# Dilated attention: queries and keys projected with their columns on partitions, instead of projected with tokens on partitions and transposed

## The reference, cut to what matters

```python
DILATED_GROUPS = ((128, 1), (512, 4), (2048, 16))   # window, dilation; N_GROUPS = 3, H_A = 16, DH_A = 64
proj = (h @ w_in).reshape(B, S, N_GROUPS, 3, H_A, DH_A)      # h: rms-normed x
for g, (window, dilation) in enumerate(DILATED_GROUPS):
    o, lse = dilated_group(proj[:, :, g, 0], proj[:, :, g, 1], proj[:, :, g, 2], bias_g, dilation, radius)
wts = jax.nn.softmax(jnp.stack(lses, axis=0), axis=0)
o = jnp.einsum('gbsh,gbshd->bshd', wts, jnp.stack(outs, axis=0))
return o.reshape(B, S, D_A) @ w_out
```

## Time and profile before

| what | value |
|---|---|
| median of 3 runs | 2387.57 us (2387.22 to 2387.86) |
| span of the profiled execution, first to last instruction | 2387.5 us (its own total time is not given; the median stands 0.1 us above this span) |
| PE busy over the span | 2351.7 us, 98% |
| DVE, ACT, POOL busy | 63%, 50%, 12% |
| granted clock of TensorE | 0.999 of full speed on the mean |
| HBM read | 408.31 MB, 171 GB/s over the span |
| matmuls of transposes for q and k in the stage (L2028) | 96 |

### The profile page before, as it was taken

How to read it: one execution, slowest core, us unless ns; L and a number is a source line. 1 busy time by engine, 2 the same in 40 slices (tenths; PEclk the granted TensorE clock), 3 DMA queues, 4 the chain that set the end, 5 groups by cost and what they waited for, 6 DMA issues and landing times.

```text
span 2387.5 us, 34279 instructions
## 1 busy us (share of the span) xinstructions
PE 2351.7 (98%) x13900; PEld 2020.1 (85%) x13900; DVE 1511.0 (63%) x2307; ACT 1195.5 (50%) x1794; POOL 283.9 (12%) x247
## 2 busy tenths in 40 slices
PE   9999999999999999999999999999999999999999
PEld 8987778779979977777899887788998887888987
DVE  6555567776555658666665677756665687656654
ACT  4444454454444446444544565555554555554543
POOL 1100010000000000000001121434110122333000
PEclk9999999999999999999999999999999999999999
DMA  7755644466566656544666654445666554445554
GB/s 229 209 194 175 172 125 136 148 187 183 186 194 177 186 185 197 173 134 151 184 186 204 203 177 143 124 126 183 186 199 206 181 170 131 121 144 172 183 189 145
DMA packets 263278, 411.66 MB, mean 172 GB/s; under 512 B 13770, under 2 KB 129370, under 8 KB 263120
## 3 DMA queue, kind: packets, MB, share of 16 engines
q1 hardware_dynamic: 256256, 389.59, 53.2%
q0 software_dynamic: 6432, 19.28, 3.1%
q10 hardware_dynamic: 432, 0.59, 0.1%
HBM read 408.31 MB, written 1.10 MB: 171 GB/s over the span
## 4 chain that ended last, share of the span: by engine, by line
PE 85%; DVE 8%; ACT 4%; issue 1%; POOL 1%; DMA 0%; SPq 0%; ACTq 0%; DVEq 0%
PE banks L1926 16%; PE banks L1928 16%; PE banks L1927 16%; PE banks L1952 9%; PE banks L1961 9%; PE banks L1953 9%; DVE w_lo L2517 2%; ACT w_hi L2205 2%; PE banks L2015 1%; PE banks L2075 1%; PE banks L2028 1%; DVE probs L2712 1%; PE banks L1909 1%; PE banks L1910 1%; PE banks L1915 1%
## 5 line engine op out<-in xcount | busy, mean ns | idle before, releaser
L2517 DVE TENSOR_TENSOR w_lo<-w_raw,w_hi 128x1024 fp32r<-128x1024 f32 x688 | 838.9, 1225 | 618.1 <-ACT w_hi L2205 616.9
L2205 ACT ACTIVATE w_hi<-w_raw 128x1024 fp32r<-128x1024 f32 (+2 forms) x744 | 777.8, 1049 | 534.6 <-PE banks L1928 379.5
L1926 PE MATMUL banks<-w_hi,xt_hi 128*128 128x512 f32 (+2 forms) x1056 | 432.3, 409 | 7.0 <-DVE xt_lo L2545 3.6
L1952 PE MATMUL banks<-xt_hi,w_hi 128*128 128x256 f32 x1728 | 426.5, 283 | 4.7 <-DVE w_lo L2517 3.1
L1953 PE MATMUL banks<-xt_hi,w_lo 128*128 128x256 f32 x1728 | 425.2, 283 | 0.0
L1928 PE MATMUL banks<-w_hi,xt_lo 128*128 128x512 f32 (+2 forms) x1056 | 413.3, 391 | 0.0
L1927 PE MATMUL banks<-w_lo,xt_hi 128*128 128x512 f32 (+2 forms) x1056 | 412.4, 391 | 0.0
L1952 PEld LDWEIGHTS banks<-xt_hi,w_hi 128*128 128x128 f32 x1728 | 326.6, 189 | 6.6 <-DVE w_lo L2517 3.4
L1953 PEld LDWEIGHTS banks<-xt_hi,w_lo 128*128 128x128 f32 x1728 | 326.7, 189 | 0.0
L1926 PEld LDWEIGHTS banks<-w_hi,xt_hi 128*128 128x128 f32 x1056 | 198.9, 188 | 52.3 <-DVE w_lo L2517 9.0
L1961 PE MATMUL banks<-xt_lo,w_hi 128*128 128x256 f32 x1728 | 243.0, 282 | 0.0
(11 more groups left out here) (438 smaller groups left out, 3042.4 us busy)
## 6 DMA issues: line engine op xcount, KB each, us to landing
w_raw<-in_w_mlp SPq DMA_DIRECT2D x128, 512.0 KB, 3.7
w_raw<-in_w_in SPq DMA_DIRECT2D x104, 512.0 KB, 3.7
w_raw<-in_ffn_w_gate SPq DMA_DIRECT2D x88, 512.0 KB, 3.9
w_raw<-in_ffn_w_up SPq DMA_DIRECT2D x88, 512.0 KB, 4.2
w_raw<-in_ffn_w_down SPq DMA_DIRECT2D x88, 512.0 KB, 3.6
w_raw<-in_attn_w_in SPq DMA_DIRECT2D x72, 512.0 KB, 3.8
w_raw<-in_ret_w_in SPq DMA_DIRECT2D x64, 512.0 KB, 3.8
w_raw<-in_ret_w_out SPq DMA_DIRECT2D x16, 512.0 KB, 3.8
```

The costliest lines, as they stand in the source:

```text
L1926: pe.matmul(bank, xh, wh, start=(c == 0), stop=False)
L1952: pe.matmul(out[f], hi[:, cols], xh, start=(c == 0), stop=False)
L2205: act.activation(k.w_hi[i % SPLIT][:, 0:m], k.raw[i % RAW][:, 0:m], ACT.Copy).then_inc(*ev.mark(k.w_hi_made, ("w_hi", i)))
L2517: dve.tensor_tensor(lo, raw, hi.bitcast(F32), ALU.subtract).then_inc(*ev.mark(k.w_lo_made, ("w_lo", i)))
```

## The change

Queries and keys of all three groups are projected with `column_pair` (two blocks of 256 columns, four tiles in all): the weights are now the stationary operand, and each tile is 24 matmuls that stream 256 tokens, so the bank holds columns on partitions and tokens along it. One bank holds a block. The row scale is then a value per element along the bank, so a 128x256 tile `row_wide` of it is made once for the stage, by PE and ACT, from the ordered row scales. The new step `evac_columns`, on DVE alone, multiplies bank by `row_wide` and writes `da_qt` (two instructions per block, with the tokens reversed inside the classes) or `da_kt` (one instruction per block). The transposes, their copies and the row buffers are gone, and the freed room holds a third pair of q/k buffers. Values are projected as before. The new evictions stand behind the split of the block's last tile in the plan; `row_order` and `row_wide` stand behind tile 3.

```diff
--- before.py
+++ after.py
@@ -669,6 +669,17 @@
             yield from self.block(xt, w, rows, start + c0, m, first, then=leave)
         return made
 
+    def column_pair(self, w, c0):
+
+        nk = TILE // SEQ
+        bs = [self.new_block(self.xt, 0, DC, SEQ) for _ in range(BLOCK // SEQ)]
+        view = w.rearrange("(k p) n -> p k n", p=P)
+        for k0 in range(0, DC, nk):
+            for n, b in enumerate(bs):
+                at = c0 + n * SEQ
+                yield from self.tile(Tile(view[:, k0:k0 + nk, at:at + SEQ], nk, SEQ, b, k0), "mm_columns")
+        return bs
+
     def pause(self, tiles, polls=16):
         until = len(self.tiles) + tiles
         for _ in range(polls):
@@ -1119,8 +1130,8 @@
         a = self.a
         self.feed(order="classes")
         self.step("masks_seen")
-        q, k = self.put("da_q", 0, [P, HALVES, D]), self.put("da_k", 8, [P, HALVES, D])
-        pairs = [(self.put(f"da_qt{n}", at, [P, DC, SEQ]), self.put(f"da_kt{n}", at + 8, [P, DC, SEQ])) for n, at in enumerate((16, 72))]
+        pairs = [(self.put(f"da_qt{n}", at, [P, DC, SEQ]), self.put(f"da_kt{n}", at + 8, [P, DC, SEQ])) for n, at in enumerate((16, 72, 0))]
+        self.row_wide_of[self.st] = self.tables[0].rearrange("p (o a) h d -> p o (a h d)", o=1)
         vs = [self.put(f"da_v{n}", 32 + 8 * n, [P, HALVES, D]) for n in range(2)]
         outs = self.da_outs = [self.tok, self.put("da_o1", 48, [P, HALVES, D])]
         heads_n = NG * H_A
@@ -1136,13 +1147,31 @@
             while any(name not in got for name in names):
                 yield IDLE
 
-        def columns(g, n, dst, after, c0):
+        def columns(g, n, c0):
+            after = got["dense"] if g == 2 else []
+
             def leave(b):
                 for half in range(HALVES):
-                    self.step("evac", Evac(b, half, self.by_turns(), dst[:, half, c0:c0 + BLOCK], list(after)))
+                    self.step("evac", Evac(b, half, self.by_turns(), vs[g % 2][:, half, c0:c0 + BLOCK], list(after)))
 
             b = yield from self.block(self.xt, w_in, D, (3 * g + n) * D + c0, BLOCK, then=leave)
-            got["qkv"[n], g, c0] = [("evac", b.uid, half) for half in range(HALVES)]
+            got["v", g, c0] = [("evac", b.uid, half) for half in range(HALVES)]
+
+        def turned_columns(g, n, c0):
+            after = [("bias_stored",)] if g == 1 else []
+            bs = yield from self.column_pair(w_in, (3 * g + n) * D + c0)
+            if not ordered:
+                order_rows()
+            for m, b in enumerate(bs):
+                self.step("evac_columns", st, b, pairs[g][n][:, (c0 + m * SEQ) // P:(c0 + (m + 1) * SEQ) // P, :], n == 0, after)
+            got["qk"[n] + "t", g, c0] = [("evac", b.uid) for b in bs]
+
+        ordered = []
+
+        def order_rows():
+            ordered.append(st)
+            self.step("row_order", st, self.new())
+            self.step("row_wide", st, [])
 
         def in_order(g, kinds):
             if g == NG - 1:
@@ -1154,42 +1183,13 @@
                 if g == NG - 1:
                     self.act_share = 3
                 for n, c0 in in_order(g, 3):
-                    after = []
-                    if n < 2 and g:
-                        yield from need(("qk"[n] + "t", g - 1, BLOCK))
-                        after = [got["qk"[n] + " read", g - 1]]
-                    if n == 2 and g == 2:
-                        yield from need("dense")
-                        after = got["dense"]
-                    yield from columns(g, n, (q, k, vs[g % 2])[n], after, c0)
+                    if n < 2:
+                        yield from turned_columns(g, n, c0)
+                    else:
+                        if g == 2:
+                            yield from need("dense")
+                        yield from columns(g, n, c0)
             self.xt_after = [self.last_tile()]
-
-        def turned(g, n, c0):
-            z, zt = (q, k)[n], pairs[g % 2][n]
-            yield from need(("qk"[n], g, c0))
-            last = (g, n, c0) == (NG - 1, 1, BLOCK)
-            if not last:
-                yield from self.pause(1)
-            after = [] if g == 0 else [("bias_stored",)]
-            if g == 2:
-                yield from need("dense")
-                after = got["dense"]
-            made = self.turn_heads(lambda half, c: z[:, half, c * P:(c + 1) * P], zt, DC // 2, got["qk"[n], g, c0], after, n == 0, first=c0 // P)
-            if last:
-                made = drive(made)
-                yield
-            else:
-                made = yield from made
-            got["qk"[n] + "t", g, c0] = made
-            got["qk"[n] + " read", g] = self.heads_read
-
-        def turns():
-            for _ in range(2):
-                yield
-            self.step("row_order", st, self.new())
-            for g in range(NG):
-                for n, c0 in in_order(g, 2):
-                    yield from turned(g, n, c0)
 
         def made(g, c0):
             return got["qt", g, c0] + got["kt", g, c0]
@@ -1220,7 +1220,7 @@
             c0, quick = first * DH_A, (g, first) == (NG - 1, OCT)
             yield from need(("qt", g, c0), ("kt", g, c0))
             at = slice(g * H_A + first, g * H_A + first + OCT)
-            o = Oct(self.new(), g, first, *pairs[g % 2], vs[g % 2], nmax[:, at, :], den[:, at, :], self.stat(2 * OCT), made(g, c0), [])
+            o = Oct(self.new(), g, first, *pairs[g], vs[g % 2], nmax[:, at, :], den[:, at, :], self.stat(2 * OCT), made(g, c0), [])
             got["oct", g, first] = o
             while before() and before().passed < 3:
                 yield IDLE
@@ -1311,7 +1311,7 @@
             yield from dense()
             yield from octs()
 
-        side = self.beside(turns(), attended())
+        side = self.beside(attended())
         drive(projections(), side, finish=False)
         self.x_read = self.xt_after[0]
         drive(self.last_normed(out_t, w_out, D, 1.0, lambda c: c in ready), side)
@@ -1964,6 +1964,34 @@
             if not last:
                 mm.then_inc(*ev.mark(k.pe_done, ("tile", i)))
 
+        if what == "mm_columns":
+            i, = of
+            t = k.tiles[i]
+            b, hi, lo = t.block, k.w_hi[i % SPLIT], k.w_lo[i % SPLIT]
+            if t.k0 == 0:
+                yield from bank_for("blk", b.uid)
+            bank = banks.held["blk", b.uid]
+            out = [bank[:, f * SEQ:(f + 1) * SEQ] for f in range(2)]
+            q.wait_ge(*(yield from ev.of("w_lo", i)))
+            for j in range(t.nk):
+                c = t.k0 + j
+                for half in range(HALVES):
+                    q.wait_ge(*(yield from ev.of(*b.xt.event_hi(half, c))))
+                xh, _ = b.xt.whole(c)
+                for f in range(2):
+                    cols = slice(j * SEQ + f * P, j * SEQ + (f + 1) * P)
+                    pe.matmul(out[f], hi[:, cols], xh, start=(c == 0 and f == 0), stop=False, skip_group_check=True)
+                    pe.matmul(out[f], lo[:, cols], xh, start=False, stop=False, skip_group_check=True)
+            for j in range(t.nk):
+                c = t.k0 + j
+                for half in range(HALVES):
+                    q.wait_ge(*(yield from ev.of(*b.xt.event(half, c))))
+                _, xl = b.xt.whole(c)
+                for f in range(2):
+                    cols = slice(j * SEQ + f * P, j * SEQ + (f + 1) * P)
+                    mm = pe.matmul(out[f], hi[:, cols], xl, start=False, stop=(c == DC - 1 and f == 1), skip_group_check=True)
+            mm.then_inc(*ev.mark(k.pe_done, *([("blk", b.uid)] if t.k0 + t.nk == DC else []), ("tile", i)))
+
         if what == "row_wide":
             st, _ = of
             bank = yield from bank_for("row_wide", st)
@@ -2561,6 +2589,25 @@
                 dve.tensor_copy(e.dst, bank[:, 0:e.block.n]).then_inc(*done)
             give_bank("blk", e.block.uid, e.half)
 
+        if what == "evac_columns":
+            st, b, dst, flip, after = of
+            bank = yield from banks.of("blk", b.uid)
+            q.wait_ge(*(yield from ev.of("blk", b.uid)))
+            q.wait_ge(*(yield from ev.of("row_wide", st)))
+            for e in after:
+                q.wait_ge(*(yield from ev.of(*e)))
+            wide = k.row_wide_of[st]
+            if flip:
+                by_class = lambda z: z.rearrange("p (c s i) -> p c s i", c=2, s=2)
+                for f in range(2):
+                    out = dst[:, f, :].rearrange("p (s c i) -> p c s i", s=2, c=2)[:, :, :, ::-1]
+                    names = [("evac", b.uid), ("bank", "blk", b.uid)] if f else [("evac_part", b.uid)]
+                    dve.tensor_tensor(out, by_class(bank[:, f * SEQ:(f + 1) * SEQ]), by_class(wide[:, 0, :]), ALU.mult).then_inc(*ev.mark(k.dve_done, *names))
+            else:
+                dve.tensor_tensor(dst, bank.rearrange("p (f t) -> p f t", f=2), wide[:, :, :].to_broadcast([P, 2, SEQ]), ALU.mult).then_inc(
```

(5 more changed lines are left out.)

## The result

The changed kernel takes 2391.3 us (median of 20 runs, 2390.8 to 2393.8), the kernel before 2388.6 in the same number of runs (2387.2 to 2389.7). The ratio is 1.0014, interval 1.0009 to 1.0020. So it is 2.7 us slower. That is clear of the noise, but within the 0.2% that I had called the same, and in the range. Its profiled execution took 2393.3 us, with a span of 2391.9, against a span of 2387.5 before.

What follows compares the result with a forecast made beforehand. PE was taken to bound the stage, with DVE's strict queue order setting its waits. 6.8 us of PE work won and given back in waits summed to +1.3 us on 2387.5, so 2388.8 us, range 2381.5 to 2393.5.

Steps and rivals of the forecast that it cites:

- wait for the row scale copy: Behind tile 3, PE waits for DVE's copy of the ordered row scales, queued behind tile 7's split: +2.3 us.
- softmax in the dense heads: Group 1: evictions come when DVE idles, so half of the one 0.9 us softmax wait goes: -0.4 us.
- first oct, scores: Group 2, behind tile 56: PE's scores come three tiles earlier and wait for DVE's k products: +4.2 us.
- first oct, values: Group 2: values wait longer for a copy on ACT, now behind both v evictions: +1.2 us.
- `combine`'s transpose: Group 2's first oct: the q eviction on DVE delaying `combine` goes, and with it the transpose's wait: -0.8 us.
- last oct, scores: Group 2, behind tile 68: k products end 3.9 us after tile 67's slot, tile 68 covers 2.8: +1.1 us.
- its values, v eviction: Last oct: values go behind tile 73, not 72, which covers the wait for the eviction of v: -1.3 us.
- ahead of tile 76: Last transposes now stand directly ahead of tile 76, which needs them; PE waits for the first low part: +2.1 us.
- The new waits: Rival: DVE is not in arrears, so the oct waits and tile 76's don't come; 2380.2 us, chance 0.20.
- The reversed write: Rival: q evictions with reversed tokens cost DVE twice the plain price, about 4.4 us on the path; 2393.2 us, chance 0.13.
- The weight loads: Rival: half as long matmuls hide weight loads less, a column tile taking 2.98 us; 2393.6 us, chance 0.02.
- The third pair: Rival, part of the forecast: third q/k buffer pair frees PE from no buffer wait, worth nothing itself, only brings octs forward.

Runs made afterwards that it cites:

- twice: Kernel before the change, with every transpose of projected queries and keys issued twice by PE: 2398.2 us, ratio 1.0041.
- all three moves: Changed kernel with rows ordered behind tile 2, copied out a tile later; group 2's first oct scores two tiles later, last oct's one: 2380.6 us, ratio 0.9968.
- filled waits: Changed kernel with unread matmuls on PE ahead of the row_wide matmuls and of the scores of group 2's first oct (a third fill never ran): 2392.5 us.

## Why the prediction was right, and where it wasn't

The forecast was 2388.8 us and no measurable difference, and it came out 2.5 us above that, inside the range. One of the 2.5 us is the base: the three runs of before that I had lie at 2387.6, the twenty at 2388.6. (The time of one execution lies about 1.3 us above its own span, 2393.3 against 2391.9 for the changed kernel; the 0.1 us that I took between median and span compared two executions.) For the change itself +1.3 us was forecast, and +2.7 came out in the medians, +4.9 in the stage of the traced executions. In kind the cause was the one given: PE wins some 6.8 us of work and gives it back in waits that the order of DVE's queue sets. In size the sum fell short, mostly by the half clock. That the result stayed in the range is owed to its width and partly to luck, since the costs of the first oct, 0.5 and 1.3 us too high, cover a part of what was missing.

| step | predicted | measured |
|---|---|---|
| transposes | -10.5 | -10.5 as work (twice: +10.5, less 0.9 hidden) |
| column tiles | +3.3 | +3.3, a tile takes 2.88 us |
| wait for the row scale copy | +2.3 | +2.3 |
| first tile | -0.3 | -0.5 (0.8 for 1.3) |
| softmax in the dense heads | -0.4 | **+1.1** (2.0 for 0.9) |
| first oct, scores | +4.2 | +3.7 |
| first oct, values | +1.2 | **-0.1**, in the other traces of this order -0.5 to +0.5 |
| `combine`'s transpose | -0.8 | -0.8 |
| last oct, scores | +1.1 | +1.0 |
| its values, v eviction | -1.3 | -1.3 |
| ahead of tile 76 | +2.1 | +1.9 |
| wait for a row scale made by POOL | not in the sum | -0.3 (0 for 0.3) |
| half clock behind waits | not in the sum | **+4.6** with three stretches, +3.1 with two |

**What held.** The work that PE wins shows in its busy time over the stage, before and in the run with all three moves, which has no half clock. It falls from 284.4 to 278.1 us, by 6.3 where 6.8 was costed:

```profile
209.05:500.81 291.76, 284.39 (x1899) 229.21 (x1899) 190.46 (x312) 144.29 (x245) 13.01 (x25) 1.00 0.51 147
207.70:492.49 284.79, 278.07 (x2384) 251.60 (x2384) 191.61 (x322) 128.81 (x212) 13.00 (x25) 1.00 0.50 151
```

The way to cost a new wait held in all four places to about 0.5 us: the engine's next slot behind the tile, plus everything that stands in DVE's queue up to the product, minus the tiles that cover it. DVE's rows behind the stretch of the earlier trace rows show it:

```profile
410.13 1.22 DVE L2545 TENSOR_TENSOR w_lo<-w_raw,w_hi 128x1024 fp32r<-128x1024 f32 x1 [0.48 <-ACT w_hi L2233]
411.28 1.41 DVE L2605 TENSOR_TENSOR da_qt<-banks,rope_q 128x256 f32<-128x256 f32 x4
412.60 2.48 DVE L2897 TENSOR_TENSOR tok<-tok,da_coef 128x512 f32<-128x512 f32 x4
...
422.10 2.35 DVE L2545 TENSOR_TENSOR w_lo<-w_raw,w_hi 128x1024 fp32r<-128x1024 f32 x2
424.37 1.28 DVE L2607 TENSOR_TENSOR da_kt<-banks,rope_q 128x512 f32<-128x512 f32 x2
```

DVE has no gap from 410.13 on, and the k products end at 425.65. The prediction had them at 426.1. Four q products occupy DVE for 1.3 us, 0.33 each, where I took 0.37. A k product takes 0.64 in a row, 0.68 alone, inside the price given.

**The rivals.** The new waits did come, all four. The reversed write is no slower than a plain one (L2605 mean 414 ns, against 417 for the same shape unreversed). The weight loads are not the bound, 2.88 us for a tile, not 2.98. The third pair is worth nothing by itself as far as the trace tells.

**What failed, step by step.** *The evictions, "I count half of it gone".* The prediction had the evictions come while DVE idles. In the changed kernel that idle time, 2.6 us here, lies ahead of the split, for which DVE waits for ACT's high part. The eviction stands behind the split and directly ahead of the maxima:

```profile
328.11 1.23 DVE L2545 TENSOR_TENSOR w_lo<-w_raw,w_hi 128x1024 fp32r<-128x1024 f32 x1 [2.59 <-ACT w_hi L2233]
329.25 1.41 DVE L2605 TENSOR_TENSOR da_qt<-banks,rope_q 128x256 f32<-128x256 f32 x4
330.58 0.62 DVE L2759 CUSTOM_DVE_ANT_1 probs<-banks,da_bias 128x256 f32<-128x256 f32 x1
```

In the trace with all three moves, three of the sixteen turns of the dense heads have an eviction pair there; they wait 0.3, 0.9 and 0.8 us, the other thirteen 0.1 at most. The prediction had named more than 2 us in total as a sign of being wrong, and it came to 2.0.

*Its values, +1.2.* The wait itself was priced about right, 1.2 + 1.2 = 2.4 us if PE is on time; what failed is that PE is on time. In the changed kernel the half clock behind the scores holds PE up by 1.5 us on its way there, and it waits 1.06. In the run with filled waits the scores are released by the same k product, but PE runs at full clock behind them, and it waits 2.27 us.

*The clock.* All waits were priced at their length. Three of them cost another 1.5 us each, because tiles behind them ran at 1.2 GHz. With this term and without the +1.2 at the values, which the second stretch fills, the sum would have been +4.6, against the +4.9 of the stage.

## What to carry to other kernels

When a step falls away, everything behind it starts earlier, on an engine that is perhaps not ready. Look for the places where PE arrives too early at a result of a loaded engine, and give exactly these consumers a tile or two of delay; here three such moves, with no change in the work, were worth 10.7 us, four times what separated the two kernels. Price a new wait on TensorE as long as the ones here (1.9 to 3.7 us) with its length and the half clock that can follow it, 1.5 us. Don't add the sizes of costs that follow each other closely: what holds PE up at one place, a wait or half clock, shortens the wait at the next.

## What was not expected of the hardware

Across the traces of this stage, TensorE ran at half its clock for 3.4 us behind all five waits of 2.3 us for the row scale copy, behind all seven of 3.7 us ahead of the first oct's scores, behind one of 2.3 us at the values, and behind five of the eight of 1.9 us ahead of tile 76; never behind one of 1.7 us or less. The fall came between 0.4 us before and 1.3 us after PE went on. With the wait of 2.3 us filled by matmuls that nobody reads (three traces), it never came, nor with the wait of 3.7 us filled (one trace). One stretch costs 1.5 us by the two executions of one kernel that differ in it. Between executions of the same program it comes and goes behind the wait of 1.9 us.
